# Expert rows scaled in place and added by PE transposes, with 24 dense keys instead of 20

## The reference, cut to what matters

```python
q = (xt @ w_q).reshape(n_tok, PEER_HEADS, 2, PEER_DKEY // 2)       # 8 heads
s = jnp.einsum('nhcd,hckd->nhck', q, sub_keys)                     # 128 keys per half
s1, i1 = lax.top_k(s[:, :, 0], 16); s2, i2 = lax.top_k(s[:, :, 1], 16)
# best 16 of the 256 sums s1 + s2; expert = i1 * 128 + i2; gates = softmax of the 16 sums
h = gelu(jnp.einsum('td,thed->the', xb, u_tab[experts]), approximate=False)
y = jnp.einsum('the,thed->td', gates * h, v_tab[experts])
x = LN(alpha * x1 + y)
```

## Time and profile before

| | us |
|---|---|
| device time, 3 runs | 1604.15, 1605.57, 1610.71 |
| median | 1605.57 |
| span of the profiled execution, first to last instruction | 1601.1 |
| median less that span | 4.5 |
| PE busy, share of the span | 1523.6, 95% |
| DVE busy | 1378.7, 86% |
| ACT busy | 605.1, 38% |
| POOL busy | 602.1, 38% |
| bytes by DMA, mean rate | 554.27 MB, 346 GB/s |

### The profile page before, as it was taken

How to read it: one execution, slowest core, us unless ns; L and a number is a source line. 1 busy time by engine, 2 the same in 40 slices (tenths; PEclk the granted TensorE clock), 3 DMA queues, 4 the chain that set the end, 5 groups by cost and what they waited for, 6 DMA issues and landing times.

```text
span 1601.1 us, 19456 instructions
## 1 busy us (share of the span) xinstructions
PE 1523.6 (95%) x6400; PEld 1000.8 (63%) x6400; DVE 1378.7 (86%) x2353; ACT 605.1 (38%) x1558; POOL 602.1 (38%) x371
## 2 busy tenths in 40 slices
PE   9999999999999989899999999989999999889896
PEld 8999899978866556455656655546665343333342
DVE  5699999775778789888989989989999988778886
ACT  5433345644322222222322322456664422222242
POOL 0000110100113234332434434535556886666662
PEclk9999999999999999999999999999999999999998
DMA  7575544385699999999999999999999999999985
GB/s 258 180 261 181 193 158 158 132 319 207 238 426 427 427 426 409 399 401 383 401 409 390 409 402 389 409 417 395 400 388 408 404 416 417 418 418 416 406 335 215
DMA packets 71060, 554.27 MB, mean 346 GB/s; under 512 B 18741, under 2 KB 19413, under 8 KB 22485
## 3 DMA queue, kind: packets, MB, share of 16 engines
q0 software_dynamic: 50560, 424.28, 64.9%
q1 hardware_dynamic: 19732, 128.61, 21.5%
q10 hardware_dynamic: 672, 0.21, 0.1%
HBM read 674.06 MB, written 4.19 MB: 424 GB/s over the span
## 4 chain that ended last, share of the span: by engine, by line
PE 36%; DMA 26%; DVE 23%; issue 10%; ACT 3%; POOL 1%; SPq 0%; POOLq 0%; DVEq 0%; ACTq 0%
DMA uv_row<-in_uv_tab,eid 14%; PE psum L867 13%; DMA uv_row<-in_uv_tab,turned 9%; DVE uv_row L1770 5%; DVE scratch L1428 4%; PE psum L560 4%; PE psum L561 4%; PE psum L562 4%; PE psum L961 4%; DVE w_lo L1356 3%; PE psum L889 3%; DVE y_last L1785 2%; DMA w_raw<-in_w_stream 1%; ACT first_key L1276 1%; DMA uv_row<-in_uv_tab,last_id 1%
## 5 line engine op out<-in xcount | busy, mean ns | idle before, releaser
L867 PE MATMUL psum<-uv_row,scratch 128*128 128x512 f32 x1432 | 670.9, 604 | 58.1 <-ACT scratch L1244 32.6
L1770 DVE CUSTOM_DVE_ANT_0 uv_row<-uv_row,x 128x2048 f32<-128x2048 f32 x256 | 585.9, 2289 | 97.5 <-DMA uv_row<-in_uv_tab,eid 47.1
L503 POOL DMA_INDIRECT uv_row<-in_uv_tab,eid x176 | 315.3, 1791 | 483.7 <-DVE y_last L1785 297.7
L867 PEld LDWEIGHTS psum<-uv_row,scratch 128*128 128x128 f32 x1432 | 264.1, 191 | 351.0 <-issue 291.8
L503 POOL DMA_INDIRECT uv_row<-in_uv_tab,turned x156 | 243.8, 1563 | 98.7 <-issue 39.3
L1222 ACT ACTIVATE dots<-dots 128x1 f32<-128x1 f32 x256 | 51.8, 202 | 604.2 <-DVE dots L1770 604.0
L560 PE MATMUL psum<-xT_hi,w_hi 128*128 128x256 f32 x640 | 183.0, 286 | 1.7 <-DVE w_lo L1356 1.2
L561 PE MATMUL psum<-xT_lo,w_hi 128*128 128x256 f32 x640 | 181.1, 283 | 0.0
L562 PE MATMUL psum<-xT_hi,w_lo 128*128 128x256 f32 x640 | 181.0, 283 | 0.0
L1356 DVE TENSOR_TENSOR w_lo<-w_raw,w_hi 128x2048 fp32r<-128x2048 f32 x62 | 141.7, 2287 | 27.6 <-ACT w_hi L1021 26.7
L921 PEld LDWEIGHTS psum<-x1T,dense_unit 128*128 128x128 f32 x640 | 121.6, 190 | 50.7 <-issue 38.3
(11 more groups left out here) (278 smaller groups left out, 1685.0 us busy)
## 6 DMA issues: line engine op xcount, KB each, us to landing
w_raw<-in_w_stream SPq DMA_DIRECT2D x63, 1024.0 KB, 4.9
dense_unit<-in_dense_u SPq DMA_DIRECT2D x20, 1024.0 KB, 11.3
dense_unit<-in_uv_tab SPq DMA_DIRECT2D x20, 1024.0 KB, 9.0
wq_first<-in_w_stream SPq DMA_DIRECT2D x8, 1024.0 KB, 11.4
wq_third<-in_w_stream SPq DMA_DIRECT2D x4, 1024.0 KB, 11.8
uv_row<-in_uv_tab,eid POOLq DMA_INDIRECT x176, 19.8
uv_row<-in_uv_tab,turned POOLq DMA_INDIRECT x156, 25.2
xT_raw<-in_xT SPq DMA_DIRECT2D x4, 512.0 KB, 5.9
```

Of the source, the lines that this page charges most:

```text
L503: pool.indirect_dma_start(dst, None, tab, bass.IndirectOffsetOnAxis(ap=ids, axis=0), bounds_check=tab.shape[0] - 1, oob_is_err=False).then ...
L867: last = pe.matmul(bank(i, n), diag[k], row[k][:, D + n * 512:D + (n + 1) * 512], start=False, stop=True, skip_group_check=True)
L1770: dve.tensor_tensor_reduce(row[k][:, 0:D], row[k][:, 0:D], x1[:, ROW_OF[s][0], :], 1.0, 0.0, ALU.mult, ALU.add, dots[:, s:s + 1]).then_inc ...
```

## The change

- `add_row` gives way to `add_turned` for steps 0 to 247 (`TOKEN_AT` = 248). ACT multiplies v in its buffer by the weight, in two pieces (two banks, then the rest), and no longer makes `diag`. PE then transposes the 16 blocks of 128 x 128 of v, accumulating in PSUM, so the banks hold features on partitions and tokens on columns. The half exchange of split rows is undone by `ident_turned` as the transposes' identity.
- All four banks of block 0, and of block 1 from `SPLIT` on, are PE's. Only for block 1's steps before `SPLIT` (`ADDED`) does DVE still add the last 512 columns into `y_last`, which `fourth_bank` transposes into the bank at `SPLIT`. `join`, `turn_last` and `y_third` are gone. The gather waits for DVE only behind such steps (`place_read`).
- `residual` multiplies by `x1T` instead of `x1`. `v_dense` uses v blocks as weights and tokens as columns: 8 products of 128 columns a part instead of 2 of 512.
- `turn_back` turns the banks to tokens on partitions again, through an ACT copy and four transposes per bank: block 0 at steps 241 and 242, block 1 at step 248, after which the last steps use `diag` with four banks.
- Block 0's four banks leave one spare bank, `side`, where there were two: dense-u, the keys' and gates' turns, the chunks and the norm products all go through it, each waiting for the copy before.
- `DENSE` is 24: 96 parts over 80 steps in dense-u, 96 over 61 in dense-v; gates and mixes are 24 wide. ACT squares 8 of a chunk's 16 tokens, and DVE compares the other 8 directly.
- `VALUES_AT` and with it `SPLIT` move from step 176 to 179, `OUT_AT` from 241 to 243.

```diff
-DENSE = 20
-DENSE_SLOT = [LATER * QUERY_PARTS + 4 + m for m in range(DENSE * PARTS)]
+DENSE = 24
+DENSE_ROWS = 80
+DENSE_SLOT = [LATER * QUERY_PARTS + 4 + DENSE_ROWS * m // (DENSE * PARTS) for m in range(DENSE * PARTS)]
+SQUARED = 8
-VALUES_AT = ROW2_AT + 1
+VALUES_AT = ROW2_AT + 4
-VALUE_ROWS = 64
+VALUE_ROWS = 61
+BACK_AT = VALUES_AT + VALUE_ROWS + 1
+OUT_AT = BACK_AT + 2
+ADDED = [s for s in range(SPLIT) if ROW_OF[s][0] == 1]
-        spare = [ps[7], ps[3]]
+        side = ps[3]
+        def pieces(s):
+            return (0, 2), (2, banks_of(s))
...
+            def place_read(s):
+                pool.wait_ge(y_done, BEFORE_IT[s] + 1)
+                if BEFORE_IT[s] in ADDED:
+                    pool.wait_ge(y_last_done, ADDED.index(BEFORE_IT[s]) + 1)
...
+            def add_turned(s):
+                i, k = ROW_OF[s][0], PLACE[s]
+                order = ident_turned if split(s) else ident
+                for part, (first, end) in enumerate(pieces(s)):
+                    pe.wait_ge(scaled, 2 * s + part + 1)
+                    for b in range(4 * first, 4 * end):
+                        last = pe.matmul(bank(i, b // 4)[:, b % 4 * P:(b % 4 + 1) * P], row[k][:, D + b * P:D + (b + 1) * P], order[:, :],
+                                         is_transpose=True, start=False, stop=True, skip_group_check=True)
+                last.then_inc(y_done, 1)
+            def fourth_bank():
+                pe.wait_ge(row2_copied, 8)
+                pe.wait_ge(y_last_done, len(ADDED))
+                for c in range(4):
+                    last = pe.matmul(bank(1, 3)[:, c * P:(c + 1) * P], y_last[:, c * P:(c + 1) * P], ident[:, :],
+                                     is_transpose=True, start=c == 0, stop=True, skip_group_check=True)
+                last.then_inc(last_turned, 1)
+            def turn_back(i, banks):
+                for n in banks:
+                    pe.wait_ge(back_copied, 4 * i + n + 1)
+                    for c in range(4):
+                        last = pe.matmul(bank(i, n)[:, c * P:(c + 1) * P], back[n % 2][:, c * P:(c + 1) * P], ident[:, :],
+                                         is_transpose=True, start=c == 0, stop=True, skip_group_check=True)
+                    last.then_inc(back_turned, 1)
...
             def v_dense(v, n):
-                for i in range(TI):
-                    last = pe.matmul(bank(i, n), mixed[:, v, i * P:(i + 1) * P], dense_unit[v % 2][:, n * 512:(n + 1) * 512],
-                                     start=v == 0 and n == PE_BANKS, stop=True, skip_group_check=True)
+                for b in range(4 * n, 4 * n + 4):
+                    for i in range(TI):
+                        last = pe.matmul(bank(i, n)[:, b % 4 * P:(b % 4 + 1) * P], dense_unit[v % 2][:, b * P:(b + 1) * P],
+                                         mixed[:, v, i * P:(i + 1) * P], start=False, stop=True, skip_group_check=True)
...
+                w = weight_turned[:, split_col(s):split_col(s) + 1] if split(s) else weight[:, s:s + 1]
+                if s >= TOKEN_AT:
...
                 if split(s):
-                    act.activation(diag[PLACE[s]], ident_turned[:, :], ACT.Identity, scale=weight_turned[:, c:c + 1]).then_inc(diag_done, 1)
+                    act.wait_ge(v_half_in[PLACE[s]], v_half_from[PLACE[s]] + 16 * SPLIT_USES[s])
+                for first, end in pieces(s):
+                    v = row[PLACE[s]][:, D + first * 512:D + end * 512]
+                    act.activation(v, v, ACT.Identity, scale=w).then_inc(scaled, 1)
...
+            def back_copy(i, n):
+                if i == 0:
+                    act.wait_ge(v_dense_done, DENSE)
+                else:
+                    act.wait_ge(y_done, TOKEN_AT)
+                if 4 * i + n >= 2:
+                    act.wait_ge(back_turned, 4 * i + n - 1)
+                act.activation(back[n % 2], bank(i, n), ACT.Copy).then_inc(back_copied, 1)
...
             def chunk(c):
-                dve.wait_ge(apart_done, c + 1)
-                dve.tensor_scalar(first_key[c % 2], first_key[c % 2], 0.0, None, ALU.is_equal)
+                dve.tensor_tensor(first_key[c % 2][:, SQUARED:, :], iota_wide.rearrange("p (o k) -> p o k", o=1).to_broadcast(wide),
+                                  first[:, SQUARED:].rearrange("p (t o) -> p t o", o=1).to_broadcast(wide), ALU.is_equal)
...
+                dve.wait_ge(apart_done, c + 1)
+                dve.tensor_scalar(first_key[c % 2][:, 0:SQUARED, :], first_key[c % 2][:, 0:SQUARED, :], 0.0, None,
+                                  ALU.is_equal).then_inc(chunk_ready, 1)
```

More of the change, by code:

```diff
@@ L57 @@
 TAIL = 2
-PE_BANKS = 3
 TAIL_BANKS = 2
+TOKEN_AT = ALL - 8
 UNITS = 3
@@ L261, in layer @@
         last_id = sb("last_id", [P, 2, TAIL], I32)
-        iota_wide_i = tmp("peer", PK).bitcast(I32)
-        diag = [tmp("peer", P) for k in range(PLACES)] + [iota_wide_i.bitcast(F32)]
         sw2_both = tmp("peer", 2 * PK)
@@ L851, in _, with residual, add_row @@
             query_turn(1)
[L853 to L857 removed]
+            def residual(i, banks):
+                for n in range(banks):
+                    pe.matmul(bank(i, n), ident_a[:, :], x1T[:, 4 * n:4 * n + 4, i * P:(i + 1) * P], start=True, stop=False,
                               skip_group_check=True)
[L860 removed]
+            def add_turned(s):
                 i, k = ROW_OF[s][0], PLACE[s]
[L863 removed]
+                order = ident_turned if split(s) else ident
[5 more added lines that the diff above has]
+                last.then_inc(y_done, 1)
+            def add_row(s, banks=4):
+                i, k = ROW_OF[s][0], PLACE[s]
+                pe.wait_ge(scaled, scaled_by(s))
                 if split(s):
@@ L987, in _ @@
                     count()
-                if s in DENSE_SLOT:
-                    dense_part(DENSE_SLOT.index(s) // PARTS, DENSE_SLOT.index(s) % PARTS)
+                for m in range(DENSE * PARTS):
+                    if s == DENSE_SLOT[m]:
+                        dense_part(m // PARTS, m % PARTS)
                 if s == IDS_AT:
-                    ids_turn()
-                if ROW2_AT <= s < ROW2_AT + 4:
-                    for m in range(2):
-                        row2_product(2 * (s - ROW2_AT) + m)
-                if GATES_AT <= s < GATES_AT + CHUNKS * CHUNK_SLOTS:
-                    chunk_part((s - GATES_AT) // CHUNK_SLOTS, (s - GATES_AT) % CHUNK_SLOTS)
+                    keys_turn()
+                if s == IDS_AT + 1:
+                    gates_turn()
+                c, slot = divmod(s - GATES_AT, CHUNK_SLOTS)
+                if 0 <= c < CHUNKS and slot:
+                    chunk_half(c, slot - 1)
                 for m in range(DENSE * PARTS):
@@ L1270, in apart @@
                     if c == 0:
-                        act.wait_ge(ids_copied, 1)
+                        act.wait_ge(ids_copied, 2)
                     if c >= 2:
                         act.wait_ge(chunk_done, c - 1)
-                for t in range(CHUNK * part // CHUNK_SLOTS, CHUNK * (part + 1) // CHUNK_SLOTS):
+                for t in range(SQUARED * part // CHUNK_SLOTS, SQUARED * (part + 1) // CHUNK_SLOTS):
                     u = c * CHUNK + t
-                    last = act.activation(first_key[c % 2][:, t, :], iota_wide, ACT.Square, bias=slot_key[1][:, u:u + 1])
+                    last = act.activation(first_key[c % 2][:, t, :], iota_wide, ACT.Square, scale=-1.0, bias=slot_key[1][:, u:u + 1])
                 if part == CHUNK_SLOTS - 1:
@@ L1307, in _ @@
                     gate_exps(r)
-                if s - 1 in DENSE_SLOT and DENSE_SLOT.index(s - 1) % PARTS == PARTS - 1:
-                    dense_copy(DENSE_SLOT.index(s - 1) // PARTS)
+                for v in range(DENSE):
+                    if s - 1 == DENSE_SLOT[v * PARTS + PARTS - 1]:
+                        dense_copy(v)
                 if s == IDS_AT + 1:
-                    ids_copy()
+                    keys_copy()
+                if s == IDS_AT + 2:
+                    gates_copy()
                 c = s - GATES_AT + CHUNK_SLOTS
@@ L1315, in _ @@
                 if ROW2_AT < s <= ROW2_AT + 4:
-                    for m in range(2):
-                        row2_copy(2 * (s - ROW2_AT - 1) + m)
+                    row2_copy(2 * (s - ROW2_AT) - 1)
+                if ROW2_AT <= s < ROW2_AT + 4:
+                    row2_copy(2 * (s - ROW2_AT))
+                if BACK_AT <= s < BACK_AT + 2:
+                    for n in range(2):
+                        back_copy(0, 2 * (s - BACK_AT) + n)
+                if s == TOKEN_AT:
+                    for n in range(4):
+                        back_copy(1, n)
                 if s == OUT_AT + 2:
@@ L1876, in _ @@
                     gates_out(0)
-                    for i in range(TI):
-                        residual_last(i)
+                    residual_last()
                 r, t = s // PACE + 1, s % PACE
```

179 lines of the change are left out of this document (82 added, 97 removed).

## The result

The changed kernel takes 1624.51 us (median of 4 runs, 1623.35 to 1631.04) against 1605.87 for the kernel before, 4 runs on the same chip: a ratio of 1.0123, with a 95% interval of 1.0099 to 1.0148. It is 1.2% slower, where 1.1% faster was forecast. The profiled execution spans 1622.2 us, 21.1 more than before; 1583 was predicted, so 39 us have to be found.

The account below looks back on a forecast made before the run. No engine was taken to bound the kernel alone: its chain alternates between PE, DMA and DVE. The terms -21 - 4 - 1 + 0 + 8 + 0 = -18 gave 1587.5 us from a median of 1605.6; range 1548 to 1640.

Parts of the forecast that it names:

- Dense-u: Rows 40 to 119, up to 1030 us: from 362 us to 341, -21, with DMA at 330 over PE 311 and DVE 315.
- -9.1 + 4.2 = -4.9: MB moved in rows 40 to 119: 9.1 fewer by gathers, 4.2 more by loads of the additional keys, net -4.9.
- Rival 1: Transfers become the only bound: rows 40 to 119 take 330 us, rows 173 to 248 take 309; 1548 us in all; chance 0.18.
- A: Rows 0 to 39, bound by transfers: 1.0 MB less to move is 2.4 us, and PE's load falls; -4 us.
- Rows 120 to 124: The five rows between the first dense stage and the chunks, bound by transfers: 0.5 MB less, -1 us.
- Chunk stage: Rows 125 to 172, to 1237 us: DVE sets it, 11.44 us per three-row chunk before and 11.42 after; change 0.
- rival 3: The clock falls to 1.2 GHz in rows 125 to 172: 17.5 us a chunk, 1685 us for all 16; chance 0.18.
- ACT's thin cover: In rows 125 to 172 ACT needs 10.2 us a chunk, leaving 1.2 us; any overdraw would cost 16 times itself.
- Rows 173 to 248: Second dense stage and the rows around it: PE becomes the bound at 333 us, 336 with waits, against 327.7 before; +8.
- 4 x 4.9: Four rows ahead of dense-v with norm products through one bank, each held by ACT's work, copies and a product: 19.6 us.
- The ending: The part after 1564.7 us, 36 us long: the same 4-bank rows and last gathers, change 0.
- Rival 4: Accumulating transposes are dearer, 0.215 us each, a row 3.44: dense-u +99, chunks 13.6 us, dense-v +99; chance 0.04.

Follow-up runs that it names:

- halfturn: The changed kernel with every second of a row's 16 transposes left out, so half of v's features never reach the sums; 1614.3 us in one run.
- shortscale: The changed kernel with ACT scaling only the first 64 columns of each piece of v, the others left unweighted; 1608.06 us in one run.
- noskip: The changed kernel gathering the dense keys' experts too, with gate zero, so no gather has missing entries; 1872.52 us in one run.
- warm1: The changed kernel plus one 256-column product of zeros on PE after each row's transposes in steps 119 to 178; 1616.22 us, ratio 1.0063 to the kernel before.
- Cast: The changed kernel with the second norm's rows spread over partitions by DMA, without eight PE products and ACT copies; 1611.27 us, ratio 1.0036 to the kernel before.

## Why the prediction was wrong

**Dense-u, predicted -21, measured -5.4: the step that failed.** "I take that as the transfers' ceiling" set 423 GB/s from a stretch of 20 us without dense loads. The 399 GB/s of dense-u was read as three engines in each other's way; it is the rate of the transfers in this stage. The change itself relieved DVE and PE, halfturn PE further, shortscale ACT, and it stayed at 398 or 399; noskip, with nothing skipped, went to 426. No run relieves DVE alone, but the queue of gathers is never empty in this stage, so it isn't DVE that holds the transfers up. At 399 GB/s the sum's own bytes give 139.5 / 0.399 = 350 us. The rest is the bytes: "-9.1 + 4.2 = -4.9" was -6.7 + 4.2 = -2.5, and 142.6 MB at 399 GB/s are 357.4 us, where 357.1 was measured. So of the miss some 8 to 9 us are rate and some 8 bytes. That PE and DVE would fall to 311 and 315 was right (313 and 314), and worth nothing. Rival 1, transfers as the only bound, had the right mechanism for this stage and the wrong rate.

**A, -4, measured +3.4.** The bytes again: the stage moved 94.9 MB before and 0.1 MB less after, where 1.0 MB less was counted, so there was next to nothing to gain. The loss is within what one execution can say: the kernels with the same A took 226.5 to 229.7 us, before 226.3. Shortscale (225.2) and halfturn (225.5) lie just under them, so a cost of 1 to 3 us by the longer hold of a buffer is possible, which the prediction saw ("Buffers are held 2 us longer by the scaling") and priced at nothing; it isn't shown. Rows 120 to 124: +1.3 for -1.

**Chunk stage, 0, measured +2.4.** Right, and for its reason: the window has DVE at 175 of 189 us. A chunk at the full clock takes 11.1 to 11.7 us, as "Sum 11.42" has it. The 2.4 are rival 3's, two chunks at half clock, and not ACT's thin cover: warm1, which scales in full and has no such chunk, takes 187.5 us. Halfturn, at half clock throughout, adds 5.6.

**Rows 173 to 248, +8, measured +18.3** (339.9 us for 321.7, by the table's dots). "So PE becomes the bound where DMA was" was right, and so was the size of dense-v's own term: 61 rows x 4.69 = 286 predicted; 1536 x 0.112 + 61 x 16 x 0.109 = 278 by the measured pitches, 277.4 by the records. Mis-sized was the stretch ahead of it. From the last narrow product to the first of dense-v the sum has 3.6 + 19.6 + 0.5 + 1.8 = 25.5 us; it took 34.3, because PE was at half clock for most of it. The waits of the single bank were in the "4 x 4.9", the clock was not. Cast, without the products and at a higher clock, took 25.5. Besides, PE came to the stretch late, by the half clock of the last chunk. The sum's 327.7 us for before include row 248, which the dots 173 to 248 leave out; up to row 249's dot it is 325.4 us before and 342.9 after, for the 336 forecast.

**The ending**, 0: right (48.0 us from row 248's dot, before and after).

**The clock, rival 3**, given 0.18, came true in part. It named the chunk stage at half clock, and there the granted clock did fall; but not all of the time (0.84, 0.65 behind it). 17.5 us was the estimate for a chunk at half clock; it took 13.0 to 13.5, since PE fell behind (69 records in the chunk shown, where a chunk has some 74) and made up for the lag at the full clock. The price of a record was right: halfturn has some 53 records a chunk, 11.6 us at twice 0.109, and ran its chunks at 195.8 / 16 = 12.2, with PE busy for 93% of them. What remained of the lag appeared where PE came out of the stage late: warm1 gives back 10.9 us, 5.9 of them behind the chunk stage. The Trainium skill ("TensorE: Matmul & The Clock Gate", Part 4) says that the full level doesn't engage for transpose mode. The trace agrees only in part. The clock fell where transposes met only 24-column products, but in halfturn it fell further, from 0.87 to 0.50, with half of the transposes gone; and dense-u, with 12 to 16 transposes a row among other products, ran at 0.98, dense-v, with 16 among 25 product records, at 1.00. Taken for every stage with transposes, the rule would have put up to 280 us on dense-u, by the prediction's own working. What the granted clock follows isn't shown by these runs.

**Rival 4** is refuted by the pitch of 0.109.

The errors sum up: 15.6 in dense-u, 7.4 in A, 2.3 and 2.4 in the next two, 10.3 in rows 173 to 248 and 1.2 before row 0: 39 us. By bytes the prediction was nearly right for the whole, -19.2 MB of gathers for -21.0, and +8.4 of dense loads for +8.4, but not for the stage where they were to pay. ACT was busy for 754 us up to the end of row 248, for "some 740".

## What to carry to other kernels

Take the rate of a transfer-bound stage from that stage, not from the best stretch nearby, and count its bytes there too: the transfers' own ceiling depends on what is gathered, and a column that is merely high in three engines doesn't prove that they hold each other up. Where work is moved onto an engine that becomes the bound, look first at the stretch ahead of it, since what that engine is late by when the stage begins goes through to the end one to one. And before a stage is explained by one execution, look at how much it differs among kernels that leave it alone: here by 3 us in A and by 7 in the chunk stage.

## What the runs showed of the hardware

- fp32 transposes that accumulate in PSUM follow one another 0.109 us apart for 128 x 128, as those that only turn do. An fp32 product with 128 columns has a pitch of 0.112 a record, nearly the same.
- The granted clock went to its lower level, 1.2 GHz, with PE's busy column at 157 of 170 us (halfturn), and stayed at 2.4 GHz in dense-v of the same kernel at 186 of 210. At the lower level 16 records of 24 columns took 3.45 us for 1.86, and a pair of 512-column product records with one partition of weights 2.07 for 1.12.
- In the same stage, indirect gathers of 16 KB rows and the same dense loads beside them moved 426 GB/s together without skipped entries and 399 with 29% of the entries skipped (7,276 rows moved of 10,240). A skipped entry leaves a packet of 4 bytes, 9 ns.
